# A conditioned hybrid decoder step: page sums begun sooner, gate products ended four steps sooner, output weights and the first tile's output products moved ahead of the last values

## The chip, the cores and the metric

The kernel runs on one core of one Trainium2 chip. The metric is device time in microseconds; three runs of the kernel before gave 1138.35 us as the median (1136.12 to 1142.52).

## What is computed

One layer of a decoder for 512 prompt tokens and 64 sample tokens (8 sequences of 8). The reference, cut to what matters here:

```python
h = rmsnorm(x, g_pre_mix) * (1 + sc1) + sh1
qa, ka, va, qb, kb, vb, logf, ga, gb = mixer_inputs(h, w_in, b_f, pos)
# sample rows, branch B: 8 heads over 2048 cached rows, kept in 16 pages of 128 per sequence
c_past = jnp.cumsum(logf_past, axis=1)
s_past = jnp.einsum('bqhe,bkhe->bhqk', q, k_past) * (e ** -0.5)
s_past = s_past + cq - jnp.transpose(c_past, (0, 2, 1))[:, :, None, :]
# both branches, prompt and sample
mix = (ga * (oa @ w_pa) + gb * (ob @ w_pb)) @ w_o
x = x + gt1 * rmsnorm(mix, g_post_mix)
h2 = rmsnorm(x, g_pre_ffn) * (1 + sc2) + sh2
x = x + gt2 * rmsnorm(hier_moe(h2, ...), g_post_ffn)     # 32 experts, two for each token
```

`ga` and `gb` are sigmoids of products of `h` with gate weights. `cumsum(logf_past)` is what this text calls the page sums: it becomes a bias that is added to the scores of branch B.

## The kernel before

Four blocks follow one another, and between two of them all engines meet. Phases A and B make the projections and the prompt's attention. Phase C is the sample attention, phase D the output projection, the router and the experts.

**Phase C** is a list of 92 steps, numbered t = 0 to 91, which every engine walks in the same order, each at its own pace, held together by semaphores. Units 0 and 3 are window attention (branch A, 7 key steps and 7 value steps), units 1 and 2 are branch B (16 and 16). A key step transposes a tile of keys on VectorE (`turn`) and multiplies it on TensorE (`score`); a value step multiplies probabilities with values (`weigh`). The order is: keys and values of unit 0 (t = 0 to 13), keys of unit 1 and four of unit 2 (14 to 33), values of unit 1 (34 to 49), keys 4 to 15 of unit 2 and four of unit 3 (50 to 65), values 0 to 11 of unit 2 (66 to 77), the last three key steps of unit 3 (78 to 80), values 12 to 15 of unit 2 (81 to 84) and the values of unit 3 (85 to 91).

Keys and values come through a ring of six slots of 1 MB. The window tiles are asked for by SyncE (`window(n)`, at t = n - 5), the pages of branch B by GpSimd. For the last 11 steps only three slots are left (`TAIL_SLOTS`), so the tile of step n is asked for when step n - 3 is done.

Between the steps stand 80 **pieces** of prompt work on TensorE: 64 half sums of the gates (4 products of 256 or 320 columns, 8 instructions in the trace) and 16 `out` pieces (the attention output times `w_pa` and `w_pb`). They are spread evenly over t = FIRST to END - 1. When they are done ScalarE copies the eight mixed tiles into `hT` (`moved`).

The **page sums** are a chain through all queues. VectorE sums along each page (`running_sums`), TensorE adds the totals of the pages before (`totals`), VectorE adds them in (`past_sums`), ScalarE's queue stores the rows in DRAM (`c_pages`), SyncE loads them in another order (`rows_c`, first storing the `terms`, for which it waits for VectorE's `scaled_terms`), ScalarE sorts them, SyncE stores `c_past`, and `past_bias` loads the first bias tiles. The first scores that need them are added by VectorE after t = 17. SUMS, the step of unit 0's first values (7), sets where in the list each link stands.

**The end of phase C and the start of D.** After the loop SyncE asks for `w_o` (4 MB, in three transfers), then `w_pa` and `w_pb` (3 MB). In phase D TensorE runs `mix(0, h)` for the two halves of the first tile of 128 rows, then the sample rows' products with `w_pa` and `w_pb` (called y below), then `mix(1, h)`, then `turn(0)`, which needs the first tile's `h2`. Phase D's own loads (x, terms, router, constants) are asked for at the start of D, and VectorE waits for all of them before its first `residual`. Each of six weight slots of the experts is refilled when an earlier expert is through.

## Time and profile before

| | |
|---|---|
| median of three runs | 1138.35 us |
| the profiled execution | 1148.97 us, its span 1147.0 us |
| TensorE busy | 989.9 us, 86% of the span |
| VectorE, ScalarE, GpSimd busy | 33%, 18%, 16% |
| granted TensorE clock, mean | 0.934 of full speed |
| DMA | 349.32 MB, mean 305 GB/s |
| phase C | from about 393 to 742 us of the span |
| phase D | from 742.7 us to the end |

The profiled execution is 10.6 us longer than the median of the runs. Times in the text are microseconds from the start of the span. A busy share is an average over stages with different limits; what counts at a place is which wait ends last there.

### The profile page before, as it was taken

Reading aid. Unit: us, or ns where it says so; the run is one execution under the profiler, and the core shown is the slowest. Engines: PE = TensorE matmul, PEld = TensorE weight load, DVE = VectorE, ACT = ScalarE, POOL = GpSimd, SP = SyncE. Lnnn points to the kernel's source line nnn. Section 1 sums busy time; section 2 is a strip of 40 time slices with the busy share of each in tenths; the row PEclk is TensorE's granted clock in tenths of the full one; section 3 lists DMA queues with packets and bytes.
Section 4 is the critical chain, followed back from the end, with each engine's and each line's share of the span. In section 5 each row is a group of like instructions: output and inputs, shape, how many; then the busy total and the mean of one; then the engine's idle time right before and its main releaser. Section 6 shows DMA issues by size and latency. Waiting matters only on the chain.

```text
span 1147.0 us, 17923 instructions
## 1 busy us (share of the span) xinstructions
PE 989.9 (86%) x7324; PEld 582.4 (51%) x7324; DVE 380.7 (33%) x877; ACT 205.8 (18%) x509; POOL 186.9 (16%) x210
## 2 busy tenths in 40 slices
PE   3999999998999699699999898699959997777770
PEld 2444444444466366476667564364545554444430
DVE  3200033215864364483057313103631230011005
ACT  3000000003445111002100212102411111111114
POOL 0000043302210103131221111000022332222110
PEclk9999999999899699799999899699959999999995
DMA  9997766787769599899999785996279999999956
GB/s 322 364 317 271 255 248 238 257 277 256 249 224 312 181 300 334 311 363 342 360 326 347 297 293 195 370 336 285 100 311 357 367 372 389 377 387 395 412 239 247
DMA packets 96845, 349.32 MB, mean 305 GB/s; under 512 B 11674, under 2 KB 55458, under 8 KB 77438
## 3 DMA queue, kind: packets, MB, share of 16 engines
q1 hardware_dynamic: 79262, 266.75, 64.8%
q0 software_dynamic: 15552, 79.97, 19.0%
q10 hardware_dynamic: 1952, 1.48, 0.5%
q8 instruction: 58, 0.95, 0.3%
q14 instruction: 21, 0.17, 0.0%
HBM read 336.31 MB, written 63.36 MB: 348 GB/s over the span
## 4 chain that ended last, share of the span: by engine, by line
PE 36%; DMA 21%; DVE 4%; SPq 2%; issue 1%; ACT 1%; ACTq 0%; DVEq 0%; POOLq 0%
DMA w_all<-in_w_exp 15%; PE bank L1632 10%; PE bank L2222 5%; PE bank L2050 4%; PE bank L1570 3%; PE bank L1508 2%; PE bank L1624 2%; PE bank L2070 2%; DVE mods L1736 1%; PE bank L1622 1%; DMA turned<-in_w_o 1%; PE bank L1493 1%; SPq L2121 1%; DMA c_pages<-w_all 1%; DMA bias<-c_pages 1%
## 5 line engine op out<-in xcount | busy, mean ns | idle before, releaser
L1632 PE MATMUL bank<-turned,w_all 128*128 128x320 f32 (+1 forms) x512 | 143.9, 425 | 3.7 <-ACT w_all L1680 3.7
L459 PE MATMUL bank<-w_all,turned 128*128 128x481 f32 (+2 forms) x384 | 119.3, 503 | 1.1 <-DVE turned L668 1.1
L459 PE MATMUL bank<-w_ring,turned 128*128 128x481 f32 (+2 forms) x384 | 118.4, 502 | 0.0
L2050 PE MATMUL bank<-w_all,mix_row 128*64 128x256 f32 x736 | 94.0, 413 | 28.3 <-DMA w_all<-in_w_exp 27.3
L1632 PEld LDWEIGHTS bank<-turned,w_all 128*128 128x128 f32 x512 | 94.4, 194 | 38.9 <-issue 18.7
L2050 PEld LDWEIGHTS bank<-w_all,mix_row 128*64 128x64 f32 x736 | 61.8, 150 | 67.5 <-issue 47.7
L1736 DVE STREAM_TRANSPOSE mods<-w_all 128x2048 f32<-128x2048 f32 (+1 forms) x39 | 86.3, 2238 | 6.6 <-DMA w_all<-in_cache_b_k,key_rows 3.2
L459 PEld LDWEIGHTS bank<-w_all,turned 128*128 128x128 f32 (+1 forms) x384 | 56.9, 172 | 61.5 <-issue 58.3
L459 PEld LDWEIGHTS bank<-w_ring,turned 128*128 128x128 f32 (+1 forms) x384 | 57.2, 172 | 60.3 <-issue 57.3
L2096 DVE COPY act_t<-bank 128x128 f32<-128x128 f32 x33 | 9.6, 292 | 199.7 <-PE bank L2060 198.0
L678 DVE COPY w_all<-bank 128x481 f32 (+5 forms) x32 | 16.9, 531 | 152.6 <-PE bank L459 152.4
L2021 POOL DMA_INDIRECT h_rows<-h,slot_rows x33 | 31.1, 943 | 138.6 <-PE bank L2036 114.7
L2222 PE MATMUL bank<-w_all,turned 128*128 128x512 f32 x96 | 44.9, 619 | 4.1 <-DMA turned<-in_w_o 4.1
L606 POOL TENSOR_TENSOR brow<-w_all,rope 128x768 f32<-128x768 f32 (+1 forms) x10 | 21.7, 2166 | 154.9 <-DVE w_all L678 151.6
L1508 PE MATMUL bank<-mods,q_b_blocks 128*32 128x128 f32 x1024 | 35.4, 280 | 13.2 <-DVE mods L1736 13.2
L1680 ACT ACTIVATE w_all<-bank 128x256 f32<-128x256 f32 x32 | 12.2, 381 | 191.1 <-PE bank L1632 191.1
L2025 POOL DMA_INDIRECT y<-h_t,slot_dest x33 | 33.8, 1024 | 77.0 <-ACT h_t L2102 76.7
L2070 PE MATMUL bank<-w_all,act_t 128*64 128x512 f32 x184 | 44.6, 605 | 0.8 <-DVE act_t L2096 0.8
L574 ACT ACTIVATE w_all<-bank 128x481 f32 (+1 forms) x16 | 9.2, 572 | 189.3 <-PE bank L459 189.3
L1468 POOL DMA_INDIRECT w_all<-in_cache_b_k,key_rows x27 | 25.4, 941 | 107.7 <-DVE mods L1736 54.9
L1468 POOL DMA_INDIRECT w_all<-in_cache_b_v,value_rows x26 | 24.3, 936 | 108.2 <-PE bank L1570 59.2
L1857 DVE SCALAR_TENSOR_TENSOR w_all<-w_all,bank 128x256 f32<-128x256 f32 x32 | 12.0, 418 | 85.2 <-PE bank L1624 85.2
(357 smaller groups left out, 1293.4 us busy)
## 6 DMA issues: line engine op xcount, KB each, us to landing
w_all<-in_w_exp SPq DMA_DIRECT2D x22, 2048.0 KB, 40.1
out_a_sample<-in_cache_a SPq DMA_DIRECT2D x8, 4080.0 KB, 21.4
w_all<-in_w_exp SPq DMA_DIRECT2D x25, 1024.0 KB, 37.8
mods<-in_w_ada SPq DMA_DIRECT2D x21, 1024.0 KB, 7.1
w_all<-in_cache_a SPq DMA_DIRECT2D x22, 512.0 KB, 7.2
turned<-in_w_exp SPq DMA_DIRECT2D x5, 2048.0 KB, 42.2
mods<-in_w_exp SPq DMA_DIRECT2D x5, 2048.0 KB, 43.5
w_all<-in_cache_a SPq DMA_DIRECT2D x36, 256.0 KB, 6.0
```

Of the source, the lines that this page charges most:

```text
L459: mm = nc.tensor.matmul(m.banks[i][r:r + ROWS[i], 0:hi - lo], m.hT[:, k, i * P:i * P + ROWS[i]], ring[u][:, CW * k + lo:CW * k + hi], star ...
L1468: pool.indirect_dma_start(out=m.ring[slot_of[n]], out_offset=None, in_=src, in_offset=bass.IndirectOffsetOnAxis(ap=rows, axis=0)).then_inc ...
L1508: mm = nc.tensor.matmul(out, m.wb[:, own(u), f, :], cols[:, f * P:(f + 1) * P], start=e == 0, stop=e == 1)
L1570: mm = nc.tensor.matmul(out[r:r + 32, :], pt[:, x % 2, h, s, 4 * c:4 * c + 4, :], v[:, 512 * c + 256 * h:512 * c + 256 * h + 256], start=x ...
L1624: mm = nc.tensor.matmul(BOTH[:, 256:512], wp_b[k][:, cols], m.obT[:, k, tokens], start=k == 0, stop=k == 3)
L1632: mm = nc.tensor.matmul(GATE[:, 0:WIDTH[h]], gate_w[b][k][:, c % 2 * P:(c % 2 + 1) * P], m.hT[:, k, 256 * h:256 * h + WIDTH[h]], start=k = ...
L1736: V.transpose(kt[:, k_num[n] % 2, 0:w].rearrange("p (f x i) -> p x f i", f=f, x=x), m.ring[slot_of[n]][:, 0:w].rearrange("p (x f j) -> p x ...
L2021: pool.indirect_dma_start(out=m.hrow[part(p), p % 2, :], out_offset=None, in_=m.h2, in_offset=bass.IndirectOffsetOnAxis(ap=at, axis=0), bo ...
L2025: pool.indirect_dma_start(out=m.y, out_offset=bass.IndirectOffsetOnAxis(ap=at, axis=0), in_=y[:, p, :], in_offset=None, bounds_check=2 * T ...
L2050: mm = nc.tensor.matmul(m.banks[2 + p][x * SLOTS:(x + 1) * SLOTS, 0:HID], hgT[:, k, :], m.weights(u)[:, (2 * k + x) * HID:(2 * k + x + 1) ...
L2070: mm = nc.tensor.matmul(m.banks[5 + p][x * SLOTS:(x + 1) * SLOTS, :], acT[:, k, :], m.weights(u)[:, c:c + 512], start=k == 0, stop=k == HI ...
L2222: mm = nc.tensor.matmul(m.banks[4 + 2 * (i % 2) + h][0:ROWS[i], :], mixT[:, k, i * P:i * P + ROWS[i]], w[:, h * 512:h * 512 + 512], start= ...
```

## The change

Four things are moved; no work is added or taken away.

1. `running_sums` goes from t = 6 to t = 3 on VectorE, `totals` and `past_sums` from t = 7 to t = 5, `scaled_terms` from t = 12 to t = 6, the store of `c_pages` on ScalarE's queue from t = 10 to t = 7, and the later links on SyncE and ScalarE by two to four steps (SUMS is 5 instead of 7).
2. The pieces are spread over t = 1 to 77 instead of 1 to 81 (the last stood at t = 80).
3. `w_o` is asked for at t = 81 of SyncE's loop, behind the window of step 86 and ahead of those of steps 87 to 91, no longer behind all of them.
4. `mix(0, h)` leaves phase D. Its 16 products stand in four groups of four (`mix_first`) behind the value steps 86 to 89, in the banks of the gates, which the pieces no longer use.

```diff
+            if (u, g) == (0, 5):
+                use(t, "after", "totals", u, 0)
...
-            if (u, g) == (0, 0):
-                use(t, "after", "totals", u, 0)
...
-    SUMS = at[(0, "v", 0)]
+    SUMS = at[(0, "v", 0)] - 2
...
-    FIRST, END = 1, 82
+    FIRST, END = 1, 78
...
+            def output_weights():
+                sp.wait_ge(mixed, 2 * KD)
+                sp.wait_ge(gate_pe, len(sums))
+                sp.wait_ge(v_used, max(v_num[n] for n in v_num if slot_of[n] in (1, 2, 3)) + 1)
+                sp.wait_ge(turned, len(k_num))
...
+                sp.dma_start(by_slot[:, 0:3, :], w_o[:, 0:3, :]).then_inc(m.wo_in, 16)
+                sp.dma_start(by_slot[:, 3:slots, :], w_o[:, 3:slots, :]).then_inc(m.wo_in, 16)
...
+                sp.dma_start(rest, w_o[:, slots:KD, :]).then_inc(m.wo_in, 16)
...
+                if t == at[(2, "v", LATE)]:
+                    output_weights()
...
-                if t == SUMS + 5:
+                if t == SUMS + 3:
                     sp.wait_ge(terms, 3)
...
-            sp.wait_ge(v_used, v_num[N - 7] + 1)
...
+            sp.wait_ge(v_used, len(v_num) - 3)
             sp.dma_start(m.slot(0)[:, 0:2 * D], I["w_pa"]).then_inc(m.wp_in, 16)
...
+            def mix_first(h, k0):
+                pe.wait_ge(moved, KD)
+                pe.wait_ge(m.wo_in, 48)
+                for k in range(k0, k0 + 4):
+                    mm = nc.tensor.matmul((GATE, BOTH)[h][:, :], m.hT[:, k, 0:P], w_o[k][:, 512 * h:512 * (h + 1)], start=k == 0, stop=k == KD - 1)
+                if k0 == 4:
+                    mm.then_inc(m.wo_pe, 1)
+
+            mix_at = {at[(3, "v", 1 + x)]: divmod(x, 2) for x in range(4)}
...
-                if t == SUMS + 3:
+                if t == SUMS + 2:
                     act.wait_ge(pre, BH + 4)
...
+                    if (u, part, g) == (0, "k", 3):
+                        running_sums()
                     if (u, part, g) == (0, "k", 6):
-                        running_sums()
                         rows_of_pages()
+                        scaled_terms()
...
             pe.wait_ge(wo_in, 16 * 3)
-            for h in range(2):
-                mix(0, h)
             pe.wait_ge(wp_in, 32)
```

What this does to the order on the engines. VectorE before, from the scores of step 5 on; the scans of `running_sums` write w_all from bias and w_all, and `past_sums` begins with the copy from a bank to bias (L1830):

```order
347 L1740 ISA w_all,chunk_max<-bank,w_all 128x256
348 L1740 ISA chunk_max 128x1
349 L1740 ISA w_all,chunk_max<-bank,w_all 128x128
350 L1740 ISA chunk_max 128x1
351 L1740 ISA w_all,chunk_max<-bank,sample_consts 128x192
352 L1740 ISA chunk_max 128x1
353 L1774 TENSOR_REDUCE neg_max<-chunk_max 128x1
354 L1819 SCALAR_TENSOR_TENSOR w_all<-bias,w_all 128x128 x8
```

VectorE with the change, from the scores of step 3 on:

```order
341 L1759 ISA w_all,chunk_max<-bank,w_all 128x256
342 L1759 ISA chunk_max 128x1
343 L1838 SCALAR_TENSOR_TENSOR w_all<-bias,w_all 128x128 x8
344 L1841 COPY bias<-w_all 128x8
345 L1843 COPY bias<-w_all 128x128
346 L1844 COPY bias<-lfn 64x128
347 L1843 COPY bias<-w_all 128x128
348 L1844 COPY bias<-lfn 64x128
349 L1755 STREAM_TRANSPOSE mods<-mods 128x8x8x32
350 L1755 STREAM_TRANSPOSE mods<-w_all 128x4x8x32
```

The scans and their copies now stand ahead of the transposes of steps 5 and 6, instead of behind the last scores of unit 0.

SyncE before, from the window of step 85 on (a window is four transfers; L278 is `window_values_in`):

```order
127 L278 DMA mods<-in_cache_a 128x2x256 x4
128 L278 DMA w_all<-in_cache_a 128x2x256 x8
129 L278 DMA mods<-in_cache_a 128x2x256 x4
130 L278 DMA w_all<-in_cache_a 128x2x256 x8
131 L278 DMA mods<-in_cache_a 128x256 x4
132 L1439 DMA w_all<-in_w_o 128x3072
133 L1440 DMA w_all<-in_w_o 128x3072
134 L1442 DMA turned<-in_w_o 128x2048
135 L1443 DMA w_all<-in_w_pa 128x2048
```

SyncE with the change:

```order
130 L279 DMA mods<-in_cache_a 128x2x256 x4
131 L279 DMA w_all<-in_cache_a 128x2x256 x4
132 L1395 DMA w_all<-in_w_o 128x3072
133 L1396 DMA w_all<-in_w_o 128x3072
134 L1398 DMA turned<-in_w_o 128x2048
135 L279 DMA w_all<-in_cache_a 128x2x256 x4
136 L279 DMA mods<-in_cache_a 128x2x256 x4
137 L279 DMA w_all<-in_cache_a 128x2x256 x8
138 L279 DMA mods<-in_cache_a 128x256 x4
139 L1448 DMA w_all<-in_w_pa 128x2048
```

The three transfers of `w_o` now stand ahead of five windows.

TensorE with the change, from the values of step 86 on (L1560 is `weigh` of unit 3, L1649 is `mix_first`, L1607 the fold of unit 2, L1532 a transpose of probabilities):

```order
534 L1560 MATMUL bank<-w_all,prob_t 32x256 x8
535 L1649 MATMUL bank<-w_all,turned 128x512 x4
536 L1607 MATMUL bank<-sample_consts,own_b 128x16 x8
537 L1532 MATMUL bank<-ident,w_all 128x128 x4
538 L1560 MATMUL bank<-w_all,prob_t 32x256 x8
539 L1649 MATMUL bank<-w_all,turned 128x512 x2
540 L1649 MATMUL bank<-turned 128x512 x2
541 L1560 MATMUL bank<-mods,prob_t 32x256 x8
542 L1649 MATMUL bank<-w_all,turned 128x512 x4
```

Before, the same rows stood there without the L1649 ones; the fold followed the values of step 86 at once.

## Rows read from the trace of the kernel before

**Rows 1.** The page, the chain that ended last: its shares by line.
```profile
DMA w_all<-in_w_exp 15%; PE bank L1632 10%; PE bank L2222 5%; PE bank L2050 4%; PE bank L1570 3%; PE bank L1508 2%; PE bank L1624 2%; PE bank L2070 2%; DVE mods L1736 1%; PE bank L1622 1%; DMA turned<-in_w_o 1%; PE bank L1493 1%; SPq L2121 1%; DMA c_pages<-w_all 1%; DMA bias<-c_pages 1%
```

**Rows 2.** Timeline of SyncE's queue after 850 us: start, us, instruction.
```profile
858.79 9.97 SPq L2121 DMA_DIRECT2D w_all<-in_w_exp  x4
```

**Rows 3.** Chain that ended last in order of time, 430 to 480 us: start, us, what.
```profile
438.10 9.83 DMA c_pages<-w_all
...
447.95 9.32 DMA bias<-c_pages
...
459.51 7.27 DMA c_past<-w_all
...
466.79 6.97 DMA bias<-c_past
```

**Rows 4.** Busy us by stretch: PE, PEld, DVE, ACT, POOL, granted clock, DMA share, GB/s.
```profile
467.00:477.00 10.00, 0.67 (x3) 0.16 (x1) 3.06 (x5) 0.50 (x2) 0.00 (x0) 0.66 0.70 218
477.00:485.00 8.00, 7.38 (x68) 5.72 (x72) 3.26 (x4) 0.00 (x0) 1.87 (x2) 0.57 0.88 279
```

**Rows 5.** Timeline of TensorE, 440 to 490 us; in brackets idle time before, and releaser.
```profile
447.96 1.89 PE L1624 MATMUL bank<-turned,w_all 128*128 128x256 f32 x8
...
465.25 2.42 PE L1632 MATMUL bank<-turned,w_all 128*128 128x320 f32 x8
477.62 1.93 PE L1508 MATMUL bank<-mods,q_b_blocks 128*32 128x128 f32 x32 [9.95 <-DVE mods L1736]
...
481.35 3.10 PE L1624 MATMUL bank<-turned,w_all 128*128 128x256 f32 x8
```

**Rows 6.** Timeline of ScalarE and its queue, 420 to 440 us.
```profile
421.92 1.09 ACT L1650 ACTIVATE prob_t<-bank 128x512 f32<-128x512 f32 x2 [0.74 <-PE bank L1527]
...
434.00 4.81 ACTq L1703 DMA_DIRECT2D c_pages<-w_all  x8
```

**Rows 7.** Timeline of VectorE, 410 to 480 us.
```profile
412.40 1.25 DVE L1736 STREAM_TRANSPOSE mods<-w_all 128x1024 f32<-128x1024 f32 x1 [0.42 <-PE bank L1493]
...
419.12 2.63 DVE L1819 TENSOR_TENSOR_SCAN w_all<-bias,w_all 128x128 f32<-128x128 f32 x8
...
473.93 0.69 DVE L1740 CUSTOM_DVE_ANT_0 w_all<-bank,bias 128x512 f32<-128x512 f32 x1 [9.83 <-DMA bias<-c_past]
```

**Rows 8.** Timeline of TensorE, 700 to 790 us.
```profile
714.19 1.93 PE L1570 MATMUL bank<-w_all,prob_t 128*32 128x256 f32 x16 [3.78 <-DMA w_all<-in_cache_b_v,value_rows]
...
740.81 1.03 PE L1597 MATMUL bank<-sample_consts,own_b 128*128 128x32 f32 x4 [0.75 <-DVE own_b L1799]
745.91 7.45 PE L2222 MATMUL bank<-w_all,turned 128*128 128x512 f32 x12 [4.07 <-DMA turned<-in_w_o]
...
754.92 5.31 PE L2222 MATMUL bank<-w_all,turned 128*128 128x512 f32 x12
...
761.78 0.55 PE L2279 MATMUL bank<-turned,w_all 128*128 128x64 f32 x4
...
786.24 1.04 PE L2259 MATMUL bank<-ident,h_rows 128*128 128x128 f32 x8
```

**Rows 9.** Timeline of SyncE's queue, 690 to 770 us.
```profile
711.64 7.43 SPq L278 DMA_DIRECT2D w_all<-in_cache_a  x8
...
732.05 0.43 SPq L1442 DMA_DIRECT2D turned<-in_w_o  x1
...
742.73 1.75 SPq L2131 DMA_DIRECT2D x<-in_x_prompt  x4
...
761.45 0.33 SPq L2144 DMA_DIRECT2D rank_consts<-in_rank_consts  x1
```

**Rows 10.** The instructions that write rank_consts, 735 to 800 us: its issue to landing.
```profile
DMA to landing us min/median/max: 10.9/10.9/10.9
```

**Rows 11.** Timeline of VectorE, 770 to 790 us.
```profile
774.40 1.41 DVE L2565 SCALAR_TENSOR_TENSOR mix_row<-bank,sums,mods 128x512 f32<-128x512 f32 x2
...
780.23 1.23 DVE L2577 TENSOR_TENSOR h_rows<-h_rows,mods 128x1024 f32<-128x1024 f32 x1
```

More of the change, by code:

```diff
@@ L132, in build @@
         m.merge_in, m.mask_in = [ctx.enter_context(nc.semaphore(n)) for n in ("merge_w", "mask_rows")]
+        m.wo_pe = ctx.enter_context(nc.semaphore("w_o_sums"))
         with ExitStack() as attn:
@@ L1384, in merge_weights @@
                 merge_weights_in(sp, I, m, p)
+            def output_weights():
[3 more added lines that the diff above has]
+                sp.wait_ge(turned, len(k_num))
+                w_o = I["w_o"].rearrange("p (k n) -> p k n", n=D)
+                slots = EXPERT_W // D
+                by_slot = m.slot(1).rearrange("p (k n) -> p k n", n=D)
+                sp.dma_start(by_slot[:, 0:3, :], w_o[:, 0:3, :]).then_inc(m.wo_in, 16)
+                sp.dma_start(by_slot[:, 3:slots, :], w_o[:, 3:slots, :]).then_inc(m.wo_in, 16)
+                rest = m.turned[:, KD * NT:KD * NT + (KD - slots) * D].rearrange("p (k n) -> p k n", n=D)
+                sp.dma_start(rest, w_o[:, slots:KD, :]).then_inc(m.wo_in, 16)
             def past_bias(u, x):
@@ L1430, in _ @@
                     sp.dma_start(ccum.rearrange("u h s k -> (u h s) k"), rows_s).then_inc(ccum_out, 16)
-            sp.wait_ge(mixed, 2 * KD)
-            sp.wait_ge(gate_pe, len(sums))
-            sp.wait_ge(v_used, max(v_num[n] for n in v_num if slot_of[n] in (1, 2, 3)) + 1)
-            sp.wait_ge(turned, len(k_num))
-            w_o = I["w_o"].rearrange("p (k n) -> p k n", n=D)
-            slots = EXPERT_W // D
-            by_slot = m.slot(1).rearrange("p (k n) -> p k n", n=D)
-            sp.wait_ge(v_used, v_num[N - 7] + 1)
-            sp.dma_start(by_slot[:, 0:3, :], w_o[:, 0:3, :]).then_inc(m.wo_in, 16)
-            sp.dma_start(by_slot[:, 3:slots, :], w_o[:, 3:slots, :]).then_inc(m.wo_in, 16)
-            rest = m.turned[:, KD * NT:KD * NT + (KD - slots) * D].rearrange("p (k n) -> p k n", n=D)
-            sp.dma_start(rest, w_o[:, slots:KD, :]).then_inc(m.wo_in, 16)
+            sp.wait_ge(v_used, len(v_num) - 3)
             sp.dma_start(m.slot(0)[:, 0:2 * D], I["w_pa"]).then_inc(m.wp_in, 16)
@@ L1635, in piece @@
                     mm.then_inc(gate_pe, 1)
+            w_o = [*(m.slot(1)[:, k * D:(k + 1) * D] for k in range(EXPERT_W // D)),
+                   *(m.turned[:, KD * NT + k * D:KD * NT + (k + 1) * D] for k in range(KD - EXPERT_W // D))]
+            def mix_first(h, k0):
[6 more added lines that the diff above has]
+            mix_at = {at[(3, "v", 1 + x)]: divmod(x, 2) for x in range(4)}
             use_pe = {"probs": probs, "shares": shares, "fold": fold, "totals": totals}
@@ L1644, in _ @@
                     (score if STEPS[t][1] == "k" else weigh)(t)
+                if t in mix_at:
+                    h, x = mix_at[t]
+                    mix_first(h, 4 * x)
                 for x in use_at.get((t, "after"), []):
@@ L1720, in _ @@
                         copy(m.hT[:, c, 0:SEQ], mix[c]).then_inc(moved, 1)
-            act.wait_ge(moved, KD)
             act.wait_ge(page_c_out, 16 * NSEQ)
@@ L1893, in _ @@
                 if t < N:
-                    if (u, part, g) == (0, "v", 5):
-                        scaled_terms()
                     if part == "v" and g + 1 == COUNT[u]:
@@ L1976, in phase_d @@
         y_pe, y_out, mixed = [sem(n) for n in ("merge", "merge_read", "mixed")]
-        wo_pe, rs, wo_out, x_ok, h_ok = [sem(n) for n in ("w_o_sums", "rstd", "w_o_read", "residual", "h2")]
+        wo_pe = m.wo_pe
+        rs, wo_out, x_ok, h_ok = [sem(n) for n in ("rstd", "w_o_read", "residual", "h2")]
         t_pe, t_d, t_a, lg_pe, lg_out, filled = [sem(n) for n in ("turned", "t_dve", "t_act", "logits", "logits_out", "filled")]
```

## Prediction

> **What bounds the kernel now.** I read the page's chain first. By its shares of lines the expert weights lead with 15%, then gate pieces and output products of TensorE [rows 1]. So the end is bound by DMA and the middle by TensorE. The question is whether time saved in the middle reaches the end. SyncE asks for the seventh expert at 858.79, when the first expert's gate products are through [rows 2]; from there the loads run one behind the other. That request hangs on TensorE, so all that comes sooner before it shifts the end with it, microsecond for microsecond.
>
> Next the chain in order of time, for the places in phase C where TensorE is not what ends a wait. There are two. The first is the page sums: c_pages, its reload, c_past, its reload, one after the other from 438.10 to 473.76 [rows 3]. VectorE sat idle for 9.83 until the first bias landed and TensorE 9.95 behind it [rows 5, 7]; in 467 to 477 it was busy 0.67 us [rows 4]. The second is the end of phase C and the start of D: 3.78 for a page, 4.07 for the output weights [rows 8].
>
> **Page sums.** No instruction is added. The chain from the first c_pages issue (434.00) to the first biased score (473.93) is 39.9 long [rows 6, 7]. I keep that length: its links are the same transfers, with the same neighbours. What moves is its start. ScalarE now issues the stores behind the probabilities of step 7, which in the trace ended at 421.92 + 1.09 = 423.0 [rows 6]. Three things in front of that are new. One more gate piece stands there (pieces are packed closer), 2.4, as the piece at 465.25 took [rows 5]. The totals' few small products now stand ahead of it, an estimated 1.8. And the scans come before the transposes of steps 5 and 6 on VectorE: 2.63 and five copies, 3.3 in all [rows 7]. The transpose of step 5 ended at 412.0 (0.42 before the one at 412.40), ahead of its use; a piece later plus 3.3 it is late. TensorE's wait there is between nothing and 3.3; I take 1.3, on an estimate that the transpose had 2 us of lead. So the stores start at 423.0 + 2.4 + 1.8 + 1.3 = 428.5 and the bias is used at 468.4.
>
> It is wanted when VectorE is free: 473.93 - 9.83 = 464.1 before, and 2.4 + 1.3 later now (the totals stood ahead of it already) = 467.8. The stall left is 0.6. It was 9.95, so 9.3 is gained. Behind the stall TensorE ran slow: granted clock 0.57 in 477 to 485 [rows 4], where eight gate products took 3.10 against 1.89 [rows 5]; that 1.2, and the same near doubling of the two groups ahead of them, is 3.0. Less the 1.3 of the new wait: **11.1 gained**. Bounds: if the chain's transfers are slowed by the page gathers, 6; if the wait at step 5 is nothing, 12.4.
>
> Moving SyncE's links costs nothing on its queue: behind the window issued at t = 8 it has none until phase C is nearly done, and only waits there. If a window stood behind the waits, it would come late by as much. ScalarE's queue is held 4.8 by the eight stores [rows 6]; the next probabilities it copies are used three steps later, which hides it.
>
> **Pieces end at step 77.** The work is the same, but three pieces (2.4, 2.4 and about 2.9, the `out` piece from its eight products in 1.89 and four more at that price [rows 5]), 7.6 in all, leave steps 78 to 80 for places where TensorE has no gap. Behind them come steps that wait for data: the page of step 84 is asked for only when step 81 is done; TensorE began step 84 at 714.19 after waiting 3.78 for it [rows 8]. Without pieces, steps 78 to 80 run at the pace of VectorE's transposes, so step 81 is done an estimated 3.7 later than before, not 7.6. **Step 84 starts at 717.9, 3.7 lost** (bounds nothing and 7.6). This and what follows is in the time of before, the 11.1 left aside.
>
> **Output weights sooner.** SyncE was through with the window of step 86 halfway in its eight transfers from 711.64 [rows 9], at 714.3 or so; now 718. Behind it come `w_o`'s 4.19 MB. Before, its last transfer was issued at 732.05 and TensorE could start at 745.91 [rows 8, 9], 13.9 later, with 1.5 MB of windows ahead. With two windows and a page ahead I take 14: they land at 732, against 745.9. TensorE reaches `mix_first` behind step 86 at about 726.6 and waits 5, and everything behind waits with it: the fold, probabilities, steps 87 to 91.
>
> From 732: four groups of 8 instructions at 5.31/12 = 0.44 each [rows 8] are 14.2; 2 for a slow clock after the wait, as 7.45 against 5.31 shows for the same instructions [rows 8]; and the rest of phase C's work, an estimated 9.6: 1.6 for the fold and probabilities of step 86, 1.0 for each of steps 87 to 91, and 3.0 for probabilities, new rows and the last fold, with the 0.75 of waiting ahead of it [rows 8]. The windows of steps 87 to 91 land behind `w_o` at about 3 us each, so 735, 738, 741, and are hidden by the mix groups. **Phase C ends at 757.8, against 741.84** (740.81 + 1.03 [rows 8]).
>
> The Trainium skill ("DMA: Bandwidth & Descriptors", the section on queues, rings and completion order) says that each DMA engine takes the descriptors of one issuing queue in ring order. That speaks against this edit: the windows can't pass the weights. The trace agrees as far as it goes, since TensorE's wait ended with the last-issued of the three. Its fixed 2.0 us plus bytes by 436 GB/s would make the weights alone 11.6, an estimate from the page; the sum above stands on the trace's 13.9.
>
> **Phase D.** Without `mix(0, h)`, which took 745.91 to 761.78, TensorE needs 786.24 - 761.78 = 24.5 to `turn(0)` [rows 8]; after a barrier of 0.9 it is there at 783.2. But `turn(0)` needs h2. VectorE's first residual began at 774.40, and h2 was there at 780.23 + 1.23 = 781.5, 7.1 later [rows 11]. It waits for D's own loads, which start at the barrier: 742.73 before, the last issued at 761.45 and landed 10.9 later [rows 9, 10], so 29.6 in all. They now start at 758.7. They have 3 MB less ahead of them (`w_pa` and `w_pb` are asked for at about 748), so I take 20: residual at 779, h2 at 786.1. Bounds: 16 (hidden, `turn(0)` at 783.2) and the old 29.6 (795.4). **`turn(0)` at 786.1 against 786.24: nothing gained, nothing lost**, bounds 3 gained and 9.2 lost. Behind `turn(0)` the order is as before.
>
> **Sum.** 11.1 + 0.1 gained on the profiled execution of 1148.97: 1137.8. The median of the runs is 10.6 below it, so 1138.35 - 11.2 = **1127.2**.
>
> **Rivals.**
> - *The loads of phase D keep their 29.6 from the barrier.* The barrier comes 16 later, `turn(0)` is at 795.4, and 9.2 of the 11.1 is lost again: 1136.5, no change that can be told (0.5%, 5.7 us, is about what can be). For it: the issuing alone takes 19 of the 29.6, and none of it is taken away. Against: the queue was full of `w_p` then. Chance 0.14.
> - *Half of the page-sum stall stays.* The stores go out while windows still land; if the chain is 5 longer, the time is 1132, on the edge. Chance 0.10.
> - *The tail hides more.* If step 84 isn't late (3.7) and the 5 of waiting for the weights is mostly filled, 5 to 8 more is gained: 1119 to 1122. Chance 0.11.
> - *Slower.* One mechanism: the barrier slips because the mix groups run at the lower of the two clock levels. The four groups would cost 28 rather than 14, the barrier would be at 773, and with 29.6 + 7.1 behind it `turn(0)` is at 810, 23 late; less 11.1 that is 12 slower, 1150. It decides once the barrier is 7 later than my 758.7, if the loads keep their length. For it: TensorE had just waited at this place before, and began slow. The Trainium skill ("TensorE: Matmul & The Clock Gate", Part 1) says that an idle TensorE falls back to 1.2 GHz and is released by sustained work; by that rule the short steps between the groups would have to wait again and again. The clock was back within the first 12 instructions in the trace [rows 8]. Chance 0.07.
>
> **How the numbers follow.** My forecast, 1122 to 1132, has 0.58. Faster by over 0.5% (below 1132.7): 0.58, 0.11, and 0.08 of the half stall: 0.77. Within: 0.14 and 0.02, 0.16. Slower: 0.07. The range for 8 in 10 leaves out the slower case and the edge of the first rival: 1119 to 1136.
>
> **What would show it.** Page sums: VectorE's wait for bias<-c_past falls from 9.83 to under 2, and a new wait of TensorE for a transpose of 1 to 2 near 415; c_pages issued 5 to 6 sooner. Tail: TensorE waits about 5 for the last `w_o` transfer behind step 86; the window waits of steps 87 to 91 are gone; phase D begins 4 to 6 later than 742.7 in its own trace (16 - 11). Phase D: `turn(0)` about 11 sooner, with a wait of some 3 for VectorE ahead of it. What would prove it wrong: the bias still late by 5 or more, or a `turn(0)` that isn't sooner.

## The result and the profile after

The changed kernel took 1162.98 us (median of four runs, 1160.69 to 1164.89) against 1137.81 for the kernel before, run beside it: ratio 1.0195, 95% interval 1.0164 to 1.0226. It is slower, and outside the range given. Run again beside its parts on another chip (15 below) the ratio was 1.0132 (1.0069 to 1.0194). The loss is real on both; its size isn't settled between the two. Part of the difference is the kernel before: its median was 1137.81 here, and 1142.51 to 1143.54 in the four sets of runs below. Every ratio in this text is to the kernel before, run beside the kernel in question.

Its profiled execution took 1160.69 (span 1158.7, mean clock 0.935). That of before was 1148.97, so the two traces differ by 11.7, where the runs differ by 25.

**The page sums: the stall went, and came back.** Timeline of TensorE of the changed kernel, 400 to 530; in brackets idle time and releaser:

```profile
416.64 1.07 PE L1498 MATMUL bank<-mods,q_a_blocks 128*32 128x256 f32 x16 [1.55 <-DVE mods L1755]
...
472.21 1.08 PE L1513 MATMUL bank<-mods,q_b_blocks 128*32 128x128 f32 x32 [1.91 <-DVE mods L1755]
...
499.92 1.99 PE L1637 MATMUL bank<-turned,w_all 128*128 128x256 f32 x8 [2.26 <-DMA w_all<-in_w_gates]
...
508.05 1.94 PE L1513 MATMUL bank<-mods,q_b_blocks 128*32 128x128 f32 x32 [6.14 <-DVE mods L1755]
...
521.79 1.08 PE L1513 MATMUL bank<-mods,q_b_blocks 128*32 128x128 f32 x32 [1.21 <-DVE chunk_max L1759]
```

The wait of 9.95 at 477.62 [rows 5] is down to 1.91, and the new wait at step 5's transpose is 1.55. The forecasts were 0.6 and 1.3. But 30 to 50 us later three waits follow that before did not have, 9.6 together, and a slow product behind the longest (1.94 against 1.08). What VectorE waited for there is a later bias tile, and this is its row, with the issue rows on SyncE's queue, the length of one issue of a bias transfer (min, median, max in ns), and the time from issue to landing of the two among those eight bias transfers whose landing the trace has:

```profile
503.67 0.69 DVE L1759 CUSTOM_DVE_ANT_0 w_all<-bank,bias 128x512 f32<-128x512 f32 x1 [11.90 <-DMA bias<-c_past]
```

```profile
466.53 0.93 SPq L263 DMA_DIRECT2D w_all<-in_w_gates  x2
469.96 5.58 SPq L1410 DMA_DIRECT2D bias<-c_past  x2
475.58 2.51 SPq L270 DMA_DIRECT2D w_all<-in_w_pa  x1
478.14 5.38 SPq L270 DMA_DIRECT2D w_all<-in_w_pb  x1
483.56 39.07 SPq L1410 DMA_DIRECT2D bias<-c_past  x6
```

```profile
L1410 SPq DMA_DIRECT2D bias<-c_past x12: 515/601/11521, 455.2 to 522.0; - x12
```

```profile
DMA to landing us min/median/max: 5.6/18.9/32.2
```

One issue usually took about half a microsecond (0.93 for two). Here it took 2.5 to 5.4, and one bias issue 11.5: SyncE itself was held. (The 39.07 spans six issues and what SyncE waited for between them.) I read this as a queue that was full. Busy time by stretch (PE, PEld, DVE, ACT, POOL, granted clock, DMA share, GB/s) shows the DMA engines at that time:

```profile
470.00:490.00 20.00, 17.77 (x238) 12.85 (x237) 18.19 (x15) 0.88 (x3) 5.77 (x7) 1.00 1.03 368
490.00:510.00 20.00, 11.60 (x127) 8.14 (x125) 7.39 (x7) 0.88 (x3) 2.65 (x3) 0.88 1.01 318
```

The DMA engines are full throughout. The same stretch of before:

```profile
470.00:490.00 20.00, 11.79 (x121) 9.08 (x122) 11.29 (x11) 0.00 (x0) 2.81 (x3) 0.66 0.81 264
```

While TensorE stood still in before, the DMA engines caught up (0.81), and the bias tiles behind the stall landed within 12.5. Whether the one is the cause of the other is what runs 6, 7, 10, 11 and 14 ask.

**The tail.** Timeline of TensorE, 715 to 800:

```profile
718.02 1.93 PE L1575 MATMUL bank<-w_all,prob_t 128*32 128x256 f32 x16 [2.96 <-DMA w_all<-in_cache_b_v,value_rows]
...
734.21 5.24 PE L1649 MATMUL bank<-w_all,turned 128*128 128x512 f32 x8 [8.92 <-DMA turned<-in_w_o]
...
759.69 0.60 PE L1602 MATMUL bank<-sample_consts,own_b 128*128 128x32 f32 x4 [0.76 <-DVE own_b L1818]
761.29 1.09 PE L2297 MATMUL bank<-turned,w_all 128*128 128x64 f32 x4 [1.00 <-PEq L1283]
762.17 1.92 PE L2299 MATMUL bank<-turned,w_all 128*128 128x64 f32 x8
...
781.80 7.04 PE L2242 MATMUL bank<-w_all,turned 128*128 128x512 f32 x12
...
797.26 1.04 PE L2279 MATMUL bank<-ident,h_rows 128*128 128x128 f32 x8
```

TensorE waits 8.92 for `w_o` behind step 86 (forecast 5). Phase D begins at 761.18, and its first work is now the products of the two branches (L2297, L2299). Eight of them take 1.92, twice the 1.06 that they take in the runs where wide products stand ahead of them; the whole lot is 20.5 (761.29 to 781.80). `turn(0)` is at 797.26 without a wait, 11.0 later than before [rows 8], and the seventh expert is asked for 11.1 later (869.87 against 858.79 [rows 2]). From there to the end the two traces take 288.8 and 288.2.

**One table for all traces.** Executions reach phase C up to 7 apart, whatever the kernel. So the times below count from the start of the first scores of phase C that waited (3.4, for VectorE; at 395.74 in before): the start of step 84, of phase D, of `turn(0)`, and the request for the seventh expert.

| kernel | step 84 | phase D | turn(0) | 7th expert | ratio to before (95%) |
|---|---|---|---|---|---|
| before | 318.5 | 347.0 | 390.5 | 463.1 | |
| before again | 318.2 | 342.5 | 387.8 | 460.3 | |
| changed | 321.7 | 364.8 | 400.9 | 473.5 | 1.0195 (1.0164, 1.0226) |
| changed again | 322.4 | 365.1 | 401.1 | 473.7 | 1.0132 (1.0069, 1.0194) |
| sums only | 321.0 | 347.4 | 393.1 | 466.6 | 1.0016 (0.9988, 1.0045) |
| pieces end at 77 only | 324.8 | 349.4 | 394.7 | 467.2 | 1.0066 (1.0044, 1.0088) |
| tail only | 316.5 | 359.5 | 395.6 | 468.2 | 1.0067 (1.0044, 1.0091) |
| changed, sums as before | 325.4 | 369.0 | 405.2 | 478.8 | 1.0136 (1.0119, 1.0153) |
| changed, mix in D | 327.3 | 363.9 | 403.7 | 476.3 | 1.0084 (1.0054, 1.0114) |
| changed, another order in D | 325.0 | 367.9 | 399.7 | 475.6 | 1.0137 (1.0107, 1.0167) |
| changed, pieces end at 81 | 321.7 | 364.6 | 400.7 | 473.3 | 1.0088 (1.0056, 1.0121) |
| changed, two bias tiles on ScalarE's queue | 328.7 | 371.9 | 408.0 | 480.5 | 1.0214 (1.0145, 1.0283) |
| sums, fewer gate weights | 314.8 | 343.4 | 386.9 | 459.3 | 0.9973 (0.9955, 0.9991) |
| before, fewer gate weights | 318.8 | 347.1 | 390.6 | 463.2 | 1.0005 (0.9985, 1.0026) |
| sums, two bias tiles on ScalarE's queue | 313.4 | 338.8 | 384.6 | 457.9 | 0.9954 (0.9916, 0.9992) |
| the same, fewer gate weights | 305.9 | 331.0 | 376.6 | 450.3 | 0.9857 (0.9816, 0.9898) |
| two bias tiles on ScalarE's queue only | 317.1 | 343.4 | 389.1 | 461.6 | 1.0004 (0.9981, 1.0028) |

How far can one trace be read? Four kernels have the changed kernel's code up to step 81 (changed, changed again, mix in D, another order in D), and they reach step 84 at 321.7, 322.4, 327.3 and 325.0. So a difference of 5 in that column says nothing by itself. Behind step 84 the traces repeat better: from there to `turn(0)` it is 78.7 to 79.7 in the six with the whole changed tail, and 69.6 to 72.1 in the nine with the old one.

### The profile page after: what moved, and what is told of

Same layout as the page of the kernel before. It is cut to its first block and busy times, and to the rows that moved or that the text cites. A ratio compares the mean times of both kernels' runs of the same rounds, so it can differ in the third digit from the quotient of the medians.

```text
span 1158.7 us, 17928 instructions
## 1 busy us (share of the span) xinstructions
PE 994.4 (86%) x7324; PEld 589.5 (51%) x7324; DVE 380.1 (33%) x877; ACT 206.2 (18%) x509; POOL 186.8 (16%) x210
## 5 line engine op out<-in xcount | busy, mean ns | idle before, releaser
L2070 PE MATMUL bank<-w_all,mix_row 128*64 128x256 f32 x736 | 94.2, 413 | 28.5 <-DMA w_all<-in_w_exp 27.4
L1513 PE MATMUL bank<-mods,q_b_blocks 128*32 128x128 f32 x1024 | 35.4, 280 | 12.7 <-DVE mods L1755 10.3
L1700 ACT ACTIVATE w_all<-bank 128x256 f32<-128x256 f32 x32 | 12.2, 381 | 191.6 <-PE bank L1637 191.6
L1473 POOL DMA_INDIRECT w_all<-in_cache_b_v,value_rows x26 | 24.3, 936 | 106.2 <-PE bank L1575 56.1
L1513 PEld LDWEIGHTS bank<-mods,q_b_blocks 128*32 128x32 f32 x1024 | 26.6, 111 | 25.4 <-DVE mods L1755 12.6
```

The lines of the kernel that those rows point to most:

```text
L1473: pool.indirect_dma_start(out=m.ring[slot_of[n]], out_offset=None, in_=src, in_offset=bass.IndirectOffsetOnAxis(ap=rows, axis=0)).then_inc ...
L1513: mm = nc.tensor.matmul(out, m.wb[:, own(u), f, :], cols[:, f * P:(f + 1) * P], start=e == 0, stop=e == 1)
L2070: mm = nc.tensor.matmul(m.banks[2 + p][x * SLOTS:(x + 1) * SLOTS, 0:HID], hgT[:, k, :], m.weights(u)[:, (2 * k + x) * HID:(2 * k + x + 1) ...
```

## The experiments

**1. The sums alone.** Kernel before, with the sums' edits (`SUMS - 2`, `totals` at step 5, stores at `SUMS + 2`, the scans and terms at their new steps).

> The kernel before with the page sums moved alone (totals behind step 5, the stores, the reload, c_past and the scans at their new places; pieces, output weights and mix as before). The changed kernel measured 25 slower than before. Theory T (tail): the loss is made behind step 84, where phase D began 18.4 later in the trace and turn(0) 11.0 later; the move of the sums costs nothing in the ordinary runs, since the stall of 9.95 is gone or was not paid there: this one at 1128 to 1140. Theory M (middle): the bias tiles that follow, now crowded on SyncE's queue with the gate weights (39 us for six issues), give it back with more: this one at 1148 or above, and a wait of TensorE of 5 or more for a biased score near 500 to 510.

Measured: no change, 1.0016 (1145.69 us, in neither theory's range). The trace is that of theory M, though the price is small. TensorE again, with SyncE's queue:

```profile
465.16 1.08 PE L1508 MATMUL bank<-mods,q_b_blocks 128*32 128x128 f32 x32 [0.69 <-DVE mods L1736]
...
499.62 3.78 PE L1632 MATMUL bank<-turned,w_all 128*128 128x256 f32 x8 [3.74 <-DMA w_all<-in_w_gates]
...
512.87 1.93 PE L1508 MATMUL bank<-mods,q_b_blocks 128*32 128x128 f32 x32 [4.93 <-DVE chunk_max L1740]
```

```profile
474.10 5.37 SPq L269 DMA_DIRECT2D w_all<-in_w_pb  x1
479.52 34.20 SPq L1396 DMA_DIRECT2D bias<-c_past  x6
513.76 1.18 SPq L262 DMA_DIRECT2D w_all<-in_w_gates  x2
```

Step by step against before, counted from the start of phase C as in the table, this kernel loses 2.0 by step 10, behind the scans, where I had allowed 1.3. Then it gains 12.2 between steps 18 and 20 (10.2 ahead) and loses 13.0 between 28 and 32 (2.8 behind), and there it stays. The bias transfers of that stretch, first their issue (min, median, max in ns), then issue to landing:

```profile
L1396 SPq DMA_DIRECT2D bias<-c_past x6: 514/1554/10335, 479.5 to 513.1; - x6
...
DMA to landing us min/median/max: 4.0/18.6/31.5
```

**2. The pieces' end alone.**

```diff
-    FIRST, END = 1, 82
+    FIRST, END = 1, 78
```

> The kernel before with the pieces ended at step 77 alone. Theory T: step 84 starts nothing to 4 later, and w_o still hangs on the late windows: 1138 to 1142. Theory M with the pieces as cause (the double piece now at step 26 delays the gate weights that SyncE asks for): 1145 or more, with a wait of TensorE for gate weights near 500.

Measured: 1.0066, 7.5 us. The gate-weight theory had the size, but the trace has no wait near 500. A late key window costs something; TensorE, VectorE's wait and SyncE's queue:

```profile
655.24 1.94 PE L1493 MATMUL bank<-mods,q_a_blocks 128*32 128x256 f32 x16 [6.21 <-DVE mods L1736]
```

```profile
652.87 2.31 DVE L1736 STREAM_TRANSPOSE mods<-mods 128x2048 f32<-128x2048 f32 x1 [9.74 <-DMA mods<-in_cache_a]
```

```profile
625.04 0.61 SPq L269 DMA_DIRECT2D w_all<-in_w_pb  x1
625.69 3.26 SPq L254 DMA_DIRECT2D w_all<-in_cache_a  x2
629.00 2.94 SPq L254 DMA_DIRECT2D mods<-in_cache_a  x2
```

Pieces packed closer ask for the last pair's gate and branch weights sooner. On SyncE's queue they now stand ahead of a key window of the last unit, which in before (second trace) was issued at 621.66 and waited for by nobody. The DMA share in 625 to 650 is 1.06. The stall of 9.95 is there as in before (10.0).

That window is the smaller part. By step 60, before it is needed, this trace is already 6.5 behind before, the price of the three pieces that now stand sooner. By step 77 it is 9.5 behind: the window added 6.21 of waiting, but a wait of 3.70 for ScalarE near step 62, which before has, is gone. Then the steps without pieces win back 3.2 by step 84, with TensorE waiting for VectorE's transposes (2.08 and 1.10 at steps 78 and 79), and 6.3 is left. Against the second trace of before the four numbers are 6.2, 9.3, 2.7 and 6.6.

**3. The changed kernel without the sums' part.**

> The changed kernel with the page sums where they were before; pieces end at 77, output weights and mix_first as changed. Theory T: the tail alone makes the loss, 1158 to 1166, and phase D's y products still run at half clock (20 us). Theory M: without the moved sums it is 1138 to 1146. If the two share it: near 1150.

Measured: 1158.65 us, in theory T's range as written; the ratio is 1.0136, as before ran at 1143.54 beside it. The branch products ran at half clock here too (20.2). With experiment 1 it says that the sums' part costs nothing that can be told by itself, and in company 0.6% by the changed kernel's first ratio or nothing by its second.

**4. The changed kernel with `mix(0, h)` in phase D.**

```diff
-                if t in mix_at:
-                    h, x = mix_at[t]
-                    mix_first(h, 4 * x)
...
+            for h in range(2):
+                mix(0, h)
```

> The changed kernel with the first tile's output products at the start of phase D again; w_o still asked for at step 81, sums sooner, pieces end at 77. Theory T with mix_first as the cause (TensorE waits 8.9 for w_o in the middle of phase C, the barrier slips, y runs at half clock): phase C ends 20 to 25 sooner, and the time is 1140 to 1150. Theory T with the order on the DMA queues as the cause (windows of steps 87 to 91 behind 4 MB of weights): steps 87 to 91 wait instead, and it stays at 1155 to 1163. Theory M: 1158 to 1163 as well, but with no wait at steps 87 to 91.

Measured: 1.0084, against 1.0195 and 1.0132 for the changed kernel. Its interval lies below that of the first and overlaps that of the second. Both tail theories have a part. From step 84 phase C takes 36.6 in place of 43.2, so it doesn't end 20 to 25 sooner, since the windows are late instead of `w_o`:

```profile
738.41 1.93 PE L1560 MATMUL bank<-w_all,prob_t 128*32 128x256 f32 x16 [9.38 <-DMA w_all<-in_cache_a]
```

That wait for step 87's window, behind 4.19 MB of weights on the same queue, takes the place of the 8.92 for `w_o`. And with `mix(0, h)` ahead of them the branch products run at full clock again (1.06 for eight).

**5. The kernel before, once more.**

> The kernel before, unchanged, profiled a second time. Its first profile took 1148.97, above all its other runs (1136 to 1146). If the stall of 9.95 for the first bias is what only the first profile had, this one shows less than 5 of it and takes some 1140; if the stall is always there, it shows 8 to 11 again, and the excess of the first profile lies elsewhere or is scatter.

Measured: 1143.92, and the stall is there (9.39), as it is in all seven traces with the sums at their old place (8.75 to 10.95). So the stall is paid in ordinary executions. The 5 us by which the first profile exceeds this one lie mostly between step 84 and phase D (28.5 against 24.3) and ahead of phase C. I take that excess for scatter.

**6 and 7. Fewer bytes, with the sums moved and without.**

```diff
+        if p:
+            hi = lo + 1
```

> The kernel before with the page sums moved, and with a quarter of the gate weights loaded for pairs 1 to 3 (one block of rows of each transfer; the products read what is there, so the gates are not the right numbers; the products themselves all stay). It takes away about 5 MB of loads in phase C, 2 to 3 MB of them between 460 and 560. Theory Q (full DMA queues): in the trace with the sums moved alone, the 15 won by step 21 are lost at steps 29 to 31 because the DMA engines are full (share 1.0) and bias and gate weights land 10 to 30 us after their issue; with fewer bytes that doesn't happen: step 32 stays 8 to 13 ahead and the time is 8 to 12 below that of sums alone, about 1133. Theory O (the order of waits on SyncE sets it, not the bytes): step 32 is where it is with the sums alone, and the time is 1140 to 1146.

> The kernel before with a quarter of the gate weights loaded for pairs 1 to 3, as in the run beside it, the page sums at their old place. Theory Q: here the stall of 9.95 stays, and the queues had drained behind it, so fewer bytes bring little, 0 to 4: 1138 to 1143. If the stall itself is made by full queues ahead of it (the bias chain slowed by other transfers), it shrinks and this one gains as much as its neighbour.

Measured: 0.9973 (0.9955, 0.9991) and 1.0005 (0.9985, 1.0026). Fewer bytes bring nothing where the stall stands (it was 10.95 in that trace), and 0.43% where it doesn't (against 1.0016 of run 1, on another chip). The wait for gate weights is gone, but that for the fourth bias tile is still there: TensorE waits 6.91 at 508.01, and a lead over before of 11.6, held from step 21 to 29, is 2.0 at step 32. The result lies between the theories; runs 10 and 11 take the question up.

**8. The order in phase D.** `mix(1, 0)` ahead of the branch products, `mix(1, 1)` behind them, in the changed kernel.

> The changed kernel with phase D's order changed: mix(1, 0), then the products of the two branches, then mix(1, 1). In the changed kernel those products stand first in phase D, and ran at half clock for 20.5 (1.92 for eight, against 1.06). Theory C (clock): they run at full clock behind eight wide products, 10.7 in all; turn(0) then hangs on h2, 7.1 behind the last constant of phase D (785.3), so it is at 792 to 793 in place of 797.3 and the time 4 to 5 below the changed kernel's: ratio to before 1.015. Theory L (loads of phase D): turn(0) stays where it is, ratio 1.0195.

Measured: 1.0137 (1.0107, 1.0167), less than the changed kernel's first ratio and no less than its second, so a gain in time isn't shown. TensorE:

```profile
761.04 7.08 PE L2242 MATMUL bank<-w_all,turned 128*128 128x512 f32 x12 [0.85 <-PEq L1283]
...
769.68 0.55 PE L2298 MATMUL bank<-turned,w_all 128*128 128x64 f32 x4
770.07 1.06 PE L2300 MATMUL bank<-turned,w_all 128*128 128x64 f32 x8
...
792.89 1.94 PE L2279 MATMUL bank<-ident,h_rows 128*128 128x128 f32 x8 [5.46 <-issue]
794.62 7.37 PE L2242 MATMUL bank<-w_all,turned 128*128 128x512 f32 x12
```

Theory C up to `turn(0)`: the branch products take 10.7 (769.68 to 780.34), and `turn(0)` is at 792.89, 4.4 ahead of the changed kernel, whose step 84 began at the same time (718.02, here 718.20). But most of it is lost at once. Behind the wait of 5.46 the clock is low again (0.50 in 793 to 797), the transposes take 1.94 for 1.04 and the twelve wide products behind them 7.37 for 5.32, and the seventh expert is asked for at 868.75, 1.1 ahead. The granted clock (sixth column of numbers, after the five engines) in the branch products, first of this run, then of the changed kernel:

```profile
770.00:780.00 10.00, 10.00 (x92) 10.00 (x91) 0.69 (x1) 0.00 (x0) 0.00 (x0) 1.00 1.00 246
```

```profile
762.00:781.00 19.00, 19.00 (x91) 19.00 (x90) 0.69 (x1) 2.55 (x8) 0.32 (x2) 0.50 1.03 278
```

The same products, at 1.00 (2.4 GHz) and 0.50 (1.2 GHz). With sixteen wide instructions in front the clock was back before the branch products began, and stayed.

**9. The changed kernel, pieces ended at step 81.**

> The changed kernel with its pieces ended at step 81 again (sums sooner, w_o asked for at step 81, mix_first behind steps 86 to 89 as changed). Ending the pieces at 77 alone cost 0.66% (7.5): in its trace the window of step 65 is asked for 7 later, at 629.0, behind the gate and branch weights of the last pair, and VectorE waits 9.74 for it. Theory A (the parts add up): this one is at 1.013 of before. Theory I (the earlier w_o needs the pieces out of the way, as it waits for them): SyncE's w_o and the windows behind it are 3 to 6 later, and it is at 1.0195 or above.

Measured: 1.0088 (1.0056, 1.0121), ten runs from 1148 to 1160. Theory A's direction, and below its 1.013. In the table its trace is like the changed kernel's: what it saves at the key window (no wait for it) it loses at the bias tile (7.64 at 518.43). The trace alone doesn't show the gain.

**10 and 11. Two bias tiles on another queue, with all bytes and with fewer.**

```diff
+                for x in (2, 3):
+                    if t == at[(1, "k", 4 * (x - 1) + 1)]:
+                        act.wait_ge(s_out, chunk_at[(1, x - 2)] + 1)
...
+                            act.dma_start(bias[:, b, :], src.unsqueeze(1).to_broadcast([16, DEC, 512])).then_inc(bias_in[b], 16)
```

> The kernel before with the page sums moved, and the third and fourth bias tiles of the first page unit (four transfers of 256 KB) issued on ScalarE's queue at the same steps, in place of SyncE's. Theory O (what holds them is SyncE's queue, full of gate and branch weights): they land within 15 of their issue in place of 31.5, VectorE doesn't wait 12.9 for them, step 31 stays 9 or more ahead, and the time is 5 to 9 below before (ratio 0.992 to 0.996), unless gate weights take the wait over. Theory Q (the DMA engines themselves are full, share 1.03): they land 20 to 30 after their issue on this queue too, and the ratio is 0.998 to 1.004.

> As the run beside it, and a quarter of the gate weights for pairs 1 to 3 (the gates are not the right numbers; all products stay). With the sums alone and so few gate weights, step 30 was 15.5 ahead and step 32 5.9, since VectorE waited 8.0 for the fourth bias tile; ratio 0.9973. Theory O: that wait goes, step 32 stays 13 ahead, ratio 0.988 to 0.991. Theory Q: it stays at 0.995 to 0.998.

Measured: 0.9954 (0.9916, 0.9992) and 0.9857 (0.9816, 0.9898). The first is in theory O's range, the second gains a little more than it said. With all bytes, ScalarE's queue and VectorE at the fourth tile:

```profile
483.21 1.18 ACTq L1708 DMA_DIRECT2D bias<-c_past  x2
```

```profile
506.27 0.65 DVE L1749 CUSTOM_DVE_ANT_0 w_all<-bank,bias 128x512 f32<-128x512 f32 x1
```

VectorE doesn't wait for it, although the DMA engines are as full as in run 1 (1.04 in 470 to 490). The trace has no landing times of these four transfers, and the fourth tile was used 23 after its issue, so that they landed within theory O's 15 isn't shown. With fewer gate weights as well, TensorE has no wait of 1 or more between steps 19 and 35, step 32 is 9.4 and 9.8 ahead of the two traces of before, the seventh expert 12.8 and 10.0, and the runs gain 1.4% (16 by the ratio, 13.6 by the medians): the whole stall and the slow products behind it. So two things on SyncE's queue gave the stall back, bias tiles behind weights, and weights that then land late. In run 10 the second was not seen; what kept it at half the gain is the first tile, for which TensorE still waited 4.93 (0.69 in experiment 1, with the same code up to there).

A rival for run 10: in those 4.93 SyncE's queue could drain, with no help from ScalarE's. Run 8 has such a trace: 4.69 of waiting for the first tile, all bias tiles on SyncE's queue, and no wait over 1.2 from there to step 50. So run 10's trace alone doesn't tell the two apart. Runs 6 and 11 do, as neither waited 1 or more for the first tile: a wait of 6.91 and 0.9973 with the tiles on SyncE's queue, no wait and 0.9857 with them on ScalarE's. The wait for the first tile itself runs from under 1 to 5.10 in the ten traces with the sums moved, and why is open. In runs 1 and 10 one link of the chain, the store of `c_past`, took 13.4 and 14.5 to land, against 7.3 in before.

**12. The same four transfers moved in the changed kernel.**

> The changed kernel with the third and fourth bias tiles of the first page unit on ScalarE's queue. In the changed kernel's trace TensorE waited 6.14 at step 29 and 2.26 for gate weights near 500, behind bias tiles that took up to 32 from issue to landing on SyncE's queue. Theory O (that queue gives the stall back): 5 to 9 of it go, ratio to before 1.012 to 1.015 against the changed kernel's in the same call. Theory E (the pieces' earlier end and the tail hold the changed kernel, whatever the middle does): within 2 of the changed kernel.

Measured: 1.0214 (1.0145, 1.0283), no gain. The bias wait is gone, and this took its place:

```profile
508.43 2.08 PE L1629 MATMUL bank<-turned,w_all 128*128 128x256 f32 x4 [4.75 <-DMA w_all<-in_w_pb]
```

With the pieces packed closer the branch weights are needed sooner, and are the next to be late (run 4, with the bias tiles on SyncE's queue, has a wait of 5.30 for them too); TensorE also waits 5.10 for the first bias and 5.86 for the late key window. Theory E in kind: no gain. Its number isn't met, since this kernel took 1163.78 against 1156.38 for the changed one beside it, with four runs each and overlapping intervals. That ScalarE's queue helps is shown only with the pieces where they were.

**13. The tail alone.**

> The kernel before with the output weights asked for at step 81 and mix_first behind steps 86 to 89, and nothing else (sums at their old place, pieces ended at step 81). Theory A (the parts add up): the three parts alone are +0.2%, +0.7% and this one, and the whole is +2.0%, so this one is at 1.009 to 1.012. Theory I (the tail costs only with the pieces ended at 77, or with the sums sooner): 1.000 to 1.005. The trace should show phase D beginning 12 to 16 later and turn(0) 7 to 10 later than before.

Measured: 1.0067 (1.0044, 1.0091), a little under theory A's 1.009. TensorE waits 8.54 for `w_o`, phase D begins 12.5 and 17.0 later than in the two traces of before, `turn(0)` 5.1 and 7.8, with the branch products at half clock:

```profile
721.67 3.75 PE L1649 MATMUL bank<-w_all,turned 128*128 128x512 f32 x4 [8.54 <-DMA turned<-in_w_o]
```

```profile
757.36 1.91 PE L2299 MATMUL bank<-turned,w_all 128*128 128x64 f32 x8
```

**14. The four transfers moved, and nothing else.**

> The kernel before with those four bias transfers on ScalarE's queue and nothing else. Theory O says that the gain of 0.46% with sums and queue together is the sums' own, freed of what gave it back; before has no wait for those tiles, so this one is at 0.999 to 1.002. The rival is that the queue alone makes the gain: 0.994 to 0.997.

Measured: 1.0004 (0.9981, 1.0028). The queue alone gains nothing, nor do fewer gate weights alone (run 7); both together with the sums at their old place were not run. So the gain of run 10 is the sums', kept.

**15. The changed kernel again.**

> The changed kernel once more, so that its parts are compared with it on one chip. Its first ratio was 1.0195 (1.0164 to 1.0226). If that holds on this chip too, 1.017 to 1.022. If chips differ in it, as the runs with the pieces ended at 81 (1.0088) suggest, 1.012 to 1.016.

Measured: 1.0132 (1.0069, 1.0194). The three parts alone add up to 0.16 + 0.66 + 0.67 = 1.5%, within the interval of this chip and short of the first one's 1.95%.

## Why the prediction was wrong

The forecast added up 11.1 gained by the sums, 3.7 lost by the pieces and 3.8 gained by the tail. The three parts alone measured 1.8, 7.5 and 7.6 lost. Each of the three terms has a step that failed.

- *Page sums, 11.1 gained.* The stall did go (9.95 to 1.91, forecast 0.6), and the new wait was 1.55 for 1.3. The step that failed is the one that let the 9.3 stand once won: it costed the moved transfers, and not what TensorE, running sooner, asks of full DMA queues. What follows was in the rows of before, had I read the stretch behind the stall (DMA share 1.0 on both sides, 0.81 inside). Net, the sums gave -2 in place of 11: a loss of 0.16% that can't be told from none. Shown by runs 1, 6, 7, 11 and 14; run 10 agrees.
- *SyncE's links cost nothing on its queue.* True of the links. But the issue rows behind them (2.5 to 5.4 for `w_pa`, `w_pb` and bias transfers, 11.5 for one) show that the queue itself was the late thing. Runs 6 and 11 show it.
- *Pieces end at 77, 3.7 lost.* Measured 7.5, and step 84 6.3 to 6.6 later (run 2). The mechanism was right in the main and its size wrong twice. Of the 7.6 moved ahead of step 78, 3.9 was to be won back by the steps without pieces; 2.7 to 3.2 was. And a term was missing: the order of weights and windows on SyncE's queue at 620 to 630, which made a key window late, for some 2 more at step 77.
- *Output weights: 5 of waiting, phase C ends 15.9 later.* `w_o` landed 14.5 after its issue, where I took 14. (The prediction's 11.6 came from a fit that the page of the Trainium skill, "DMA: Bandwidth & Descriptors", gives for transfers issued by GpSimd; `w_o` is SyncE's, and the measurement decides.) The wait was 8.92, as TensorE was at `mix_first` at 725.3, 7.3 behind the start of step 84, where I had taken 8.7, and the issue came a little later. From the start of step 84 to that of phase D: forecast 40.8, measured 43.2 (43.0 alone). Right in mechanism, 2 to 3 too small.
- *Phase D: `turn(0)` hangs on h2.* Wrong. Forecast 27.4 from phase D's start to `turn(0)`, measured 36.1, and no wait. The term that failed is the 24.5 for what stands between, taken from rows in which `mix(0, h)` had first brought the clock back. It measured 36.0: the branch products took 20.5 for 10.7, and the first twelve wide ones behind them 7.04 for 5.31. I had put the low clock (0.07) on the mix groups; those ran at full speed but for the first, and the narrow products in phase D paid. Run 8 shows it, and shows too that most of what the full clock gives there is lost again behind `turn(0)`. The loads of phase D landed 24 after its start (20 forecast), hidden. In before, too, they weren't alone in holding h2: the last constant landed at 772.3, and VectorE's last wait ahead of its residual was for the branch products:

```profile
772.65 0.69 DVE L2538 SCALAR_TENSOR_TENSOR w_all<-w_all,bank 128x512 f32<-128x512 f32 x1 [4.67 <-PE bank L2281]
```

- *Sum.* Forecast from step 84 to `turn(0)` 68.2, against 72.0 before; measured 79.2, against 72.0 and 69.6. So the tail is 7 to 10 slower than before, where I had it 3.8 faster.
- *The rivals.* The slower one (0.07, 1150) had the right kind and the wrong place; none had the time. The half stall that stays was in effect a whole one that came back. The ring-order rule of the Trainium skill ("DMA: Bandwidth & Descriptors", queues and ring order) I used for windows behind `w_o`, and it applied as well to bias tiles behind weights; the gain of another queue from run 6 to run 11 agrees with it. The clock rule that I weighed ("TensorE: Matmul & The Clock Gate", Part 1, of the Trainium skill) speaks of sustained work. The wide products agree; the branch products don't, which kept TensorE busy from 761.29 to 781.80 at 0.50.

What stays open: why the ratio was 1.0195 on one chip and 1.0132 on the other (the intervals overlap; before was about 5 faster on the first chip than on the others), and why the traces of changed and before differ by 12 while the runs beside them differ by 25. The traces of before are of 1148.97 and 1143.92 among runs from 1136 to 1149.

The version that beats both kernels is run 10's: sums sooner, two bias tiles on ScalarE's queue, pieces and tail as before. It is 0.5% faster (0.08 to 0.84%), at the edge of what can be told. Run 11, whose gates are not the right numbers, says that 1.4% is there for whoever gets the gate weights out of the way too.

## What to carry to other kernels

A stall of a compute engine can also be the time in which its DMA queues drain. Before counting its removal as gain, read the DMA share and the issue-to-landing times behind it: where the share is 1.0 on both sides, ask which transfer is late next, and whether small urgent transfers stand behind large patient ones on one queue. And when long products are moved away from the front of a stage, price what is left there at the lower clock.

## What the runs showed of the hardware

- Behind weights on the same queue a transfer's issue can itself be held: up to 10.3 for one of 256 KB in run 1 and 11.5 in the changed kernel, where 0.5 to 0.6 is usual. Four such transfers from another engine's queue were issued in 0.53 to 0.63 each (run 10), at a DMA share of 1.04, and nothing waited for the fourth tile. A full share alone doesn't hold the issues: in run 8 at 1.04 in 470 to 490 none took over 1.0.
- A transfer that was issued without delay can still land late: in run 6 each bias issue took under 0.9, and the slowest landed 30.5 later.
- Narrow products (64 columns) ran at a granted clock of 0.50 for 20 us on end, behind pauses of 0.76 and 1.00 (761.29 to 781.80), though TensorE was busy all the time, with products and with weight loads; wide ones (512 columns) reached the full rate within the first twelve (7.04 and then 5.31 for the same twelve). The same narrow products, begun at 1.00, kept it for all of their 10.7 (run 8).
